# Joints between stages: norms, memory attention and a convolution re-ordered in a two-block transformer kernel

## The reference

```python
# first block
h = rmsnorm(x); q, k, v, gate = h @ w_in                 # two attentions of 8 heads each
y = [rmsnorm(forgetting_attention), rmsnorm(chunked_relpos_attention)]
x = x + rmsnorm(y @ w_out)
x = x + rmsnorm(softmax((rmsnorm(x) @ w_mq) K^T / 16) V @ w_mo)   # K, V from rmsnorm(mem), 256 rows, 4 heads
x = x + rmsnorm(square(relu(rmsnorm(x) @ w_ff1)) @ w_ff2)
# second block; c gives shift, scale and gate of every step (mod = silu(c) @ ada_w + ada_b)
h = modulate(rmsnorm(x)); a, g = split(h @ conv_in)
u = a * sigmoid(g); y = depthwise_conv(u, 31 taps) + b
x = x + gate * (silu(layer_norm(y)) @ conv_out)
x = x + gate * (square(relu(modulate(rmsnorm(x)) @ mlp1)) @ mlp2)
x = x + gate * hgrn2_mixer(modulate(rmsnorm(x)))         # gated linear recurrence, both directions
x = x + gate * (square(relu(...)) @ mlp2)
return rmsnorm(x)
```

## Time and profile before

| what | value |
|---|---|
| median of 3 runs | 2250.37 us (2248.27 to 2253.09) |
| profiled execution | 2249.68 us, its span 2247.7 us |
| PE busy | 2123.1 us (94%), 10732 matmuls |
| DVE / ACT / POOL busy | 1246.2 / 833.7 / 231.3 us |
| mean granted clock of PE | 0.983 |

### The profile page before, as it was taken

The page is one execution under the profiler, slowest core; times in us unless marked ns, Lnnn a source line. Parts: engine busy times, 40 slices in busy tenths (PEclk is TensorE's granted clock), DMA queues, the critical chain, the costliest instruction groups (busy, mean ns, idle before and its releaser), DMA issues.

```text
span 2247.7 us, 26801 instructions
## 1 busy us (share of the span) xinstructions
PE 2123.1 (94%) x10732; PEld 1658.6 (74%) x10732; DVE 1246.2 (55%) x1864; ACT 833.7 (37%) x1334; POOL 231.3 (10%) x189
## 2 busy tenths in 40 slices
PE   6999898899899999896999999999999989999998
PEld 5777786676778776563788888877767767888886
DVE  4455655427676776785553343456666665443443
ACT  4344544335332332313442232344454543332232
POOL 2221104014000003342100000100000001000001
PEclk9999999999999999998999999999999999999999
DMA  5212321122776773364232322221211132222321
GB/s 171 75 57 94 110 97 59 54 75 96 260 243 221 264 247 120 96 148 113 75 100 95 106 94 94 75 70 48 66 57 51 54 100 88 94 94 94 112 94 38
DMA packets 217531, 241.75 MB, mean 108 GB/s; under 512 B 9920, under 2 KB 203968, under 8 KB 211264
## 3 DMA queue, kind: packets, MB, share of 16 engines
q1 hardware_dynamic: 207232, 229.03, 31.3%
q10 hardware_dynamic: 10176, 11.00, 2.0%
HBM read 229.01 MB, written 2.10 MB: 103 GB/s over the span
## 4 chain that ended last, share of the span: by engine, by line
PE 80%; DVE 9%; ACT 6%; issue 2%; ACTq 1%; DMA 1%; POOL 1%; DVEq 0%; POOLq 0%
PE bank L1070 22%; PE bank L1071 21%; PE bank L1072 21%; PE bank L1091 2%; PE bank L1092 2%; PE bank L1093 2%; DVE wL L1636 1%; ACTq L1483 1%; PE bank L1263 1%; PE bank L1240 1%; PE bank L1196 1%; PE bank L1141 1%; DVE aacc L1804 1%; PE bank L1154 1%; ACT L1283 1%
## 5 line engine op out<-in xcount | busy, mean ns | idle before, releaser
L1070 PE MATMUL bank<-hH,wH 128*128 128x512 f32 (+1 forms) x1672 | 667.0, 399 | 41.0 <-DVE hL L1642 16.0
L1071 PE MATMUL bank<-hL,wH 128*128 128x512 f32 (+1 forms) x1672 | 649.8, 389 | 0.0
L1072 PE MATMUL bank<-hH,wL 128*128 128x512 f32 (+1 forms) x1672 | 649.7, 389 | 0.0
L1636 DVE TENSOR_TENSOR wL<-raw,wH 128x1024 fp32r<-128x1024 f32 (+1 forms) x342 | 384.6, 1166 | 162.3 <-ACT wH L1299 162.2
L1299 ACT ACTIVATE wH<-raw 128x1024 fp32r<-128x1024 f32 (+1 forms) x378 | 335.1, 937 | 373.9 <-PE bank L1072 279.8
L1070 PEld LDWEIGHTS bank<-hH,wH 128*128 128x128 f32 x1672 | 317.2, 190 | 136.9 <-issue 53.7
L1072 PEld LDWEIGHTS bank<-hH,wL 128*128 128x128 f32 x1672 | 317.2, 190 | 65.2
L1071 PEld LDWEIGHTS bank<-hL,wH 128*128 128x128 f32 x1672 | 317.4, 190 | 62.8 <-issue 2.9
L1070 PE MATMUL bank<-hidH,wH 128*128 128x512 f32 x768 | 300.5, 391 | 7.7 <-DVE hidL L1784 7.7
L1071 PE MATMUL bank<-hidL,wH 128*128 128x512 f32 x768 | 299.8, 390 | 0.0
L1072 PE MATMUL bank<-hidH,wL 128*128 128x512 f32 x768 | 299.7, 390 | 0.0
(11 more groups left out here) (204 smaller groups left out, 2072.0 us busy)
## 6 DMA issues: line engine op xcount, KB each, us to landing
raw<-in_mlp SPq DMA_DIRECT2D x64, 1024.0 KB, 5.3
araw<-in_ada_w SPq DMA_DIRECT2D x48, 1024.0 KB, 5.0
raw<-in_w_ff SPq DMA_DIRECT2D x32, 1024.0 KB, 7.3
raw<-in_hgrn_in SPq DMA_DIRECT2D x32, 512.0 KB, 3.8
raw<-in_w_in SPq DMA_DIRECT2D x12, 1024.0 KB, 5.3
u<-uc ACTq DMA_DIRECT2D x128, 67.5 KB, 3.3
raw<-in_conv_in SPq DMA_DIRECT2D x16, 512.0 KB, 4.8
raw<-in_w_mv SPq DMA_DIRECT2D x4, 1024.0 KB, 6.0
```

Of the source, the lines that this page charges most:

```text
L1070: mm(out, wh[:, k, m:m + 128], xh[:, k, 0:width], start=k == 0, stop=False)
L1071: mm(out, wh[:, k, m:m + 128], xl[:, k, 0:width], start=False, stop=False)
L1072: i = mm(out, wl[:, k, m:m + 128], xh[:, k, 0:width], start=False, stop=k == KB - 1)
L1636: e.tensor_tensor(wL[:, s, c], raw[:, r, c], wH[:, s, c].bitcast(F), SUB).then_inc(*s_wlo.up(n, x))
```

## The change

The parts, in the order of the list:

- *Memory squares.* The loads of mem and the eight squares with their additions stand before the k6 layer; the high and low parts stay behind it.
- *w_out and w_mo.* The last output block is squared from its bank. In `post_pre` all additions to x are on DVE; squares of blocks 0 to 3 are added by DVE between, those of 4 to 7 by POOL once the next layer has been asked for (`beside`).
- *Groups.* `fresh` is now a number; mq, ff1, mlp1, mlp2 and conv_out work their first four blocks (two pieces) together; the second piece's `take` does not look ahead. `hold=5` instead of 4 puts the norm's sum behind five blocks.
- *Memory attention.* A unit enters at each step (`stagger(..., 1)`) instead of four at a time.
- *First feed-forward.* A hidden block's low part is an item of its own, put behind the next block's first steps where several are pending; RM is 0.47 and the conditioning begins at -12.
- *Norm after the first feed-forward.* The root goes to a PSUM bank; four of the blocks are scaled into banks and added by DVE, blocks 0, 2, 4, 5 are added by POOL.
- *Convolution.* a and g of block 0 are worked together. For the last block half of the shifted copies are issued by SP, and only three DVE taps stand before the sum of block 6. The mean is of seven blocks; they are centred on it (0 to 2 by DVE, 3 to 6 by POOL) and squared before the eighth is there; the eighth is centred on the same mean, its sum (`rest`) corrects variance and blocks.

```diff
-RW, RM = 1.4, 0.44
+BY_POOL = (0, 2, 4, 5)
+RW, RM = 1.4, 0.47
-    def take(self, name, k0, c0, nc_):
+    def take(self, name, k0, c0, nc_, ahead=True):
...
-        while self.made < n + NSPLIT:
+        while ahead and self.made < n + NSPLIT:
...
+    def last_low(self):
+
+        if self.hidden is not None:
+            self.do("hidden_lo", **self.hidden)
+            self.hidden = None
...
+            group = fresh if c == 0 and fresh else 1
+            span = max(nc_, 128 * group)
+            ns = [self.take(name, k0, c0 + c + x, nc_, ahead=x == 0) for x in range(0, span, nc_)]
+            if self.beside is not None:
+                self.beside()
+                self.beside = None
...
+        if nxt is None:
+            rb, free = self.lin.get()
+            self.close(tag, 1024, busy=BUSY, out=(rb, free))
+            for j in range(KB):
+                pool = j in BY_POOL
+                z, free = (None, ()) if pool else self.lin.get()
+                self.do("post", tag=tag, src=src, j=j, rb=rb, z=z, after=free)
+                self.do("post_x", tag=tag, src=src, j=j, pool=pool, z=z)
...
+        else:
+            self.close(tag, 1024, busy=BUSY)
+            add = {}
+            for j in range(KB):
+                self.do("post", tag=tag, src=src, j=j, rb=None, z=None)
+                if j:
+                    self.do("pre_lo", tag=tag, nxt=nxt, j=j - 1)
+                self.do("post_x", tag=tag, src=src, j=j, pool=False, z=None)
+                self.do("pre_hi", tag=tag, nxt=nxt, j=j)
+                if j < 4:
+                    self.to_add = None
+                    self.square(nxt, j, ("xT", j), (self.x_event(tag, j),), by="dve")
+                    add[j + 2], self.to_add = self.to_add, None
+                if add.get(j) is not None:
+                    self.do("add_square", **add[j])
...
-                                   fresh=q == 0, hold=4)
+                                   fresh=4 if q == 0 else 0, hold=5)
...
+            for j in range(4):
+                do("mem", j=j)
+            yield from mem_squares()
             yield from self.linear("k6", "w_in", 0, 2312, 256, src, to_k(6), lag=True)
             yield from mem_kv()
...
+                if j == KB - 1:
+                    self.square(tag, j, ("bank", b), (("mm", "lin", t, j),), last=True)
                 do("ev_block", tag=tag, lin=t, j=j, b=b)
...
-        run(pipeline((munit(h, i) for h in range(4) for i in range(4)), 4))
+        run(stagger((munit(h, i) for h in range(4) for i in range(4)), 1))
...
-        run(weave(self.ffn("ff_pre", "w_ff1", 0, "w_ff2", 0, ("h", "ff_pre"), True, to_y), ada(), RM, start=-6.0))
+        run(weave(self.ffn("ff_pre", "w_ff1", 0, "w_ff2", 0, ("h", "ff_pre"), True, to_y), ada(), RM, start=-12.0))
...
+        def both():
+
+            ns = [self.take("conv_in", 0, c, 128, ahead=c == 0) for c in (0, 1024)]
+            parts = []
+            for n, t in zip(ns, "ag"):
+                b, free = self.lin.get()
+                parts.append(dict(n=n, m=0, b=b, after=free, key=("lin", (t, 0), 0), j=0))
...
+            else:
+                do("wdiag", blk=blk, k0=conv_first(blk), slot=slots[blk], after=free)
+                both()
             do("shift", blk=blk, slot=slots[blk], after=free)
             if blk:
                 b = taps_pe(blk - 1)
-            taps_dve(blk, range(5))
+            early = 5 if blk < KB - 1 else 3
+            taps_dve(blk, range(early))
...
+        taps_dve(KB - 1, range(3, conv_first(KB - 1)))
+        last = taps_pe(KB - 1)
+        vb, vfree = self.lin.get()
...
+        for j in (0, 3, 1, 4, 2, 5, 6):
+            do("ln_centre", j=j, s=s, pool=j > 2)
+            square_of(j)
+        do("conv_sum", blk=KB - 1, b=last, taps=conv_first(KB - 1))
...
+        do("ln_rest", b=db, after=free)
+        square_of(KB - 1)
+        do("ln_rest_square", b=db, s2=s2, free=free2)
+        do("ln_root", b=vb, s2=s2, rstd_free=self.rstd_free)
...
-                    for s in range(4):
+                    for s in range(4) if blk < KB - 1 else (0, 1):
...
+                elif kind == "shift" and it["blk"] == KB - 1:
...
+                    for s in (2, 3):
+                        for g in range(4):
+                            dma(u4[32 * s:32 * s + 32, x, g, :], uc[32 * g:32 * g + 32, blk, s:s + T + 28]).then_inc(
+                                s_u4[x], LANDED)
```

More of the change, by code:

```diff
@@ L205, in lows, with linear @@
         self.owed.clear()
-    def linear(self, tag, name, k0, c0, ncols, src, ev, width=T, nc_=256, before=None, lag=False, fresh=False, hold=1):
+    def linear(self, tag, name, k0, c0, ncols, src, ev, width=T, nc_=256, before=None, lag=False, fresh=0, hold=1):
         late = []
@@ L233, in linear @@
                         self.lows()
-                if m0 + 128 * group >= nc_:
-                    self.piece_done[n] = parts[-1]["key"]
+                for x, n in enumerate(ns):
+                    if m0 < nc_ * (x + 1) <= m0 + 128 * group:
+                        self.piece_done[n] = parts[-1]["key"]
                 if before is not None and len(late) + len(parts) >= hold:
@@ L270, in linear_tm, with square @@
                 yield 1.0
-    def square(self, tag, j, blk, after, last=False):
+    def square(self, tag, j, blk, after, last=False, by="pool"):
         if last:
@@ L419, in post_pre, with rest @@
             self.do("pre_lo", tag=tag, nxt=nxt, j=KB - 1)
-            for j in range(KB):
-                self.square(nxt, j, ("xT", j), (self.x_event(tag, j),))
+            def rest():
+                for j in range(4, KB):
+                    self.square(nxt, j, ("xT", j), (self.x_event(tag, j),))
+            self.beside = rest
         self.rstd_free = (("dve", "post", tag, KB - 1),)
     def x_event(self, tag, j):
-        ends = {"mix_post": True, "mem_post": True, "ff_post": False}
@@ L426, in x_event @@
-        if tag not in ends:
-            return ("dve", "x", tag, j)
-        pool = j > 0 if ends[tag] else j % 2 == 0
+        pool = tag == "ff_post" and j in BY_POOL
         return ("pool" if pool else "dve", "x", tag, j)
@@ L521, in to_gate @@
             return (("dve", "gate", 1),)
-        run(self.linear("q0", "w_in", 0, 0, 256, src, to_q(0), before=close_first, fresh=True, hold=2))
+        run(self.linear("q0", "w_in", 0, 0, 256, src, to_q(0), before=close_first, fresh=2, hold=2))
         run(self.linear("gate", "w_in", 0, 1536, 128, src, to_gate, nc_=128))
@@ L576, in ev @@
             def ev(t, j, b):
+                if j == KB - 1:
+                    self.square(tag, j, ("bank", b), (("mm", "lin", t, j),), last=True)
                 do("ev_block", tag=tag, lin=t, j=j, b=b)
-                self.square(tag, j, ("ymix", j), (("act", "y", tag, j),), last=j == KB - 1)
+                if j < KB - 1:
+                    self.square(tag, j, ("ymix", j), (("act", "y", tag, j),))
                 return (("act", "y", tag, j),)
             return ev
-        run(self.linear("w_out", "w_out", 0, 0, 1024, ("h", "y"), to_block("mix_post"), fresh=True))
+        run(self.linear("w_out", "w_out", 0, 0, 1024, ("h", "y"), to_block("mix_post"), fresh=2))
         self.post_pre("mix_post", "mem_pre", "ymix")
@@ L1201, in tensor_program @@
                         pe.wait_ge(*event(ev))
-                    mm(banks[it["b"]][:], ones, nacc[:], start=True, stop=False).then_inc(*s_mm.up("mean0"))
-                    pe.wait_ge(*s_dve.at("c", KB - 1))
-                    mm(banks[it["b"]][:], ones, yc[:, KB - 1, :], start=False, stop=True).then_inc(*s_mm.up("mean"))
+                    mm(banks[it["b"]][:], ones, nacc[:], start=True, stop=True).then_inc(*s_mm.up("mean"))
+                elif kind == "ln_rest":
+                    pe.wait_ge(*s_dve.at("cen", KB - 1))
+                    mm(banks[it["b"]][:], ones, yc[:, KB - 1, :], start=True, stop=True).then_inc(*s_mm.up("rest"))
                 elif kind == "ln_var":
+                    if it["first"]:
+                        for ev in it["after"]:
+                            pe.wait_ge(*event(ev))
                     pe.wait_ge(*s_act.at("csq", it["j"]))
-                    mm(banks[it["b"]][:], ones, tmp[:, it["s2"], :], start=it["j"] == 0, stop=it["j"] == KB - 1).then_inc(
+                    mm(banks[it["b"]][:], ones, tmp[:, it["s2"], :], start=it["first"], stop=it["last"]).then_inc(
                         *s_mm.up("var", it["j"]))
@@ L1868, in vector_program @@
                         *s_dve.up("c", blk))
-                elif kind == "ln_var":
+                elif kind == "ln_centre" and not it["pool"]:
                     j = it["j"]
@@ L2000, in pool_program @@
                             *s_wlo_pool.up(n, x))
-                elif kind == "square" and it["add"] is not None:
+                elif kind == "square" and it["add"] is not None and it["by"] == "pool":
                     pool.wait_ge(*s_act.at("sq", it["tag"], it["j"]))
```

247 lines of the change are left out of this document (155 added, 92 removed).

## The result

The changed kernel takes 2220.33 us (median of 4 runs, 2218.75 to 2221.82), the kernel before beside it 2251.73 (2248.27 to 2254.62): ratio 0.9861, 95% interval 0.9843 to 0.9879, so 31 us less. 2215 was forecast, in a range of 2203 to 2231. The profiled execution spans 2220.0 us at a mean clock of 0.982, against 2247.7.

A forecast was written before the change was run, and what follows sets the result against it. TensorE, busy 94% of the span, was taken as the bound, so only fewer matmuls or less standing and 1.2 GHz time help. Terms summed to 35.6 us off 2249.68: 2214.1, with 0.7 to the median 2215; range 2203 to 2231.

The forecast's parts named there:

- Memory squares: Before k6: squares and adds done under k6's matmuls remove TensorE's 6.84 us wait; gain 5.5 us, bounds 3 and 8.
- the 3 us that I took off: Behind k6: late copies to high and low parts and the attention step cost about 3 us of wait.
- Norms: After w_out and w_mo: no GpSimd additions, groups of four banks, TensorE sets the pace; net 6.0 us each, 12.0 together.
- Attention: Memory attention: one row entering per step lets scores cover the softmax, heads of 9.0 us; gain 7.0, bounds 3 and 9.
- With start=-12 ... gain 6.0: First feed-forward, first quarter's joint: conditioning begins after the quarter's 20 steps, removing two hidL waits of 3.0 us each.
- The surplus reappearing at three joints, 1.5 us: Later feed-forward quarters: 0.47 a step instead of 0.44 raises VectorE's demand; loss 1.5 us (0 to 8).
- the late sum: End of first feed-forward: last conditioning sum, its copy and DMA issues delay the norm's logarithm on ScalarE; loss 1.8 us.
- Rival B: First feed-forward: VectorE becomes the bound under 0.47, three joints of 3 to 5 us, norms low; 2230 us, chance 0.18.
- Outer norm: Norm after first feed-forward: VectorE operations with an operand in PSUM are not held up by GpSimd; gain 4.2 us.
- Start of the convolution: Block 0: g1's parts come behind 16 copy issues on ScalarE, TensorE stands 10 us; net -5.5 instead of +3.9.
- End of the convolution: Last block: copies from two queues 5.5 us sooner, norm 13.6 instead of 17.9 us; gain 9.7, bounds 5 and 12.
- rival C: Convolution: after the 10 us stand the clock stays at 1.2 GHz until its end; 77 us, 2292 us, chance 0.02.

The follow-up runs named there:

- the last run: Changed kernel with g1 asked for ahead of the copies, conditioning from -8.2, and mem's loads ahead of q6 (also "that with three"): 2201.4 us, ratio 0.9779.
- the version with two edits: Changed kernel with g1 asked for ahead of the copies and conditioning at 0.47 a step from -8.2 instead of -12: 2204.26 us, ratio 0.9782.

## Why the prediction was right, point by point

- *Memory squares*: right, 5.7 for 5.5, shown by the run that undoes them. What stays is not what I named (copies behind k6) but ScalarE's stand for the loads, which I had called harmless to TensorE; they cost 1 to 2 us, and some 2 more where the half clock follows. So the 3 us that I took off are met by luck, by another wait (2.2 us for PTb and the half clock behind it).
- *Norms*: 12.7 with the shortened w_out and w_mo stretches, for 12.0. Without the groups of four the gain of 5.6 a norm is gone, and taking the additions from GpSimd gives 0.1; whether the groups need that new order is not shown, as they were not run without it. Of "no hL waits" two are left, 1.15 us each at the first block. The 1.2 us for the logarithm was 0.8.
- *Attention*: right. A head takes 8.8 us, as forecast within 0.2 (3.5 + 0.9 + 3.5 is 7.9, not 7.8). The 8.5 us for 7.0 hold a phase of half clock that only the kernel before has; with it taken off the gain is 6.7.
- *First feed-forward*: the step that failed. "With start=-12 ... gain 6.0" gives nothing once the low parts come a block later, and that edit, which I did not cost, makes 5.4 of the 8.7 us. My 6.0 counted the two waits alone (2.96 and 2.91 us); the other 2.8 are the half clock that came with them (0.51 from 569 to 576 in the kernel before). "The surplus reappearing at three joints, 1.5 us" was 5.2, and not by density alone: the waits for aacc grew from 2.5 to 6.6 us, and behind both the clock was low (0.66 from 704 to 709 and from 810 to 815), some 1.6 us each, for which I had no term. At the same 0.47, started 3.8 earlier, 2.8 of the 5.2 go (4.3 where the clock stayed up, in the last run), and so does the late sum. Rival B's mechanism was at work here, at less than its price. The errors cancel, which is luck: 3.5 for 4.5.
- *Outer norm*: 3.3 for 4.2 (from the exponential's end at 866.91 to the logarithm at 878.01 are 11.1 us, forecast 10.1). Products and additions end at 875.21, after 8.3 us for 8.2 forecast; it is the tail that takes 2.8 us for 1.8, because the last blocks come together: three squares queue on ScalarE and six sums on TensorE, at a granted clock of 1.00 and 0.43 us a sum. Operands in PSUM make 3.0 of the gain, shown. The late sum was 1.4 for 1.8.

```profile
874.45 1.67 ACT L1428 ACTIVATE tmp<-xT 128x512 f32<-128x512 f32 x3 [0.66 <-POOL xT L2159]
...
875.13 2.84 PE L1206 MATMUL bank<-tmp,cst 128*128 128x512 f32 x6 [0.17 <-ACT tmp L1428]
```

- *Start of the convolution*: right in mechanism, place and size, -5.7 for -5.5, shown from both sides.
- *End of the convolution*: the norm 4.3 as forecast; the copies 4.1 for 5.5 (the stretch is 11.2 to 13.2 us in the other executions with two queues, so 3.2 to 5.2). SyncE does issue in 0.65 us like ScalarE; it was the landing that I had at about 2 us behind the last issue, where it is 4.7, although already had 4.3. The seven subtractions took 6.4 us on both engines together, between the prediction's 4.3 and 7.0 (VectorE's three took 1.36 us each, where one without GpSimd beside it takes 0.69), and as forecast that stayed under the conv matmuls.

```profile
1017.18 4.07 DVE L1988 TENSOR_TENSOR yc<-yc,tmp 128x512 f32<-128x512 f32 x3 [1.06 <-ACT tmp L1586]
1017.23 6.39 POOL L2170 TENSOR_TENSOR yc<-yc,tmp 128x512 f32<-128x512 f32 x4 [2.90 <-ACT tmp L1586]
```

- *Clock*: rival C did not come about; g1 ran at half clock for some 5 us, and block 6 was level again.

## What to carry to other kernels

A look-ahead that is switched off for one piece moves that piece's preparation to wherever the next request stands in its engine's queue: look at what is issued in between, DMA issues most of all. Work that is interleaved by steps moves when a loop is regrouped, even if its pace stays, so set its start anew. Two edits against the same stand overlap: undo each by itself before giving it a share.

## What the runs showed of the hardware

In a dense stretch, in which TensorE was busy for 20 of the 20 us before, the granted clock fell to 1.2 GHz for eight matmuls in one execution and stayed at 2.4 GHz at the same matmuls in another. First the changed kernel, then the kernel before (length, PE, PEld, DVE, ACT, POOL busy, clock, DMA share, GB/s):

```profile
60.00:80.00 20.00, 20.00 (x112) 16.42 (x111) 4.04 (x6) 4.67 (x8) 0.53 (x2) 1.00 0.35 105
80.00:90.00 10.00, 10.00 (x39) 7.58 (x38) 7.00 (x17) 3.59 (x10) 5.67 (x5) 0.83 0.35 106
```

```profile
60.00:80.00 20.00, 20.00 (x105) 16.09 (x104) 5.36 (x11) 5.93 (x9) 2.27 (x4) 1.00 0.27 85
80.00:90.00 10.00, 10.00 (x46) 7.22 (x45) 8.19 (x19) 2.15 (x10) 6.51 (x5) 1.00 0.35 106
```

Each such phase costs 1.5 to 1.7 us, and the executions differ in how many they have (matmul 1000 at 183.9 to 191.7). The same holds behind short stands. In the version with two edits and in that with three, TensorE stands 2.65 us for the same sum of the conditioning, and then has the low clock in the one and not in the other:

```profile
788.00:793.00 5.00, 4.46 (x16) 2.72 (x17) 2.35 (x4) 1.74 (x3) 0.00 (x0) 0.66 0.70 240
```

```profile
789.00:794.00 5.00, 4.47 (x23) 3.07 (x24) 2.35 (x4) 1.75 (x3) 0.00 (x0) 1.00 0.71 233
```

The Trainium skill, "TensorE: Matmul & The Clock Gate", HAM oscillation, ties the low clock to stands of TensorE between dense pieces; the stands of 9.3 us here bear that out each time, those of 1.7 to 2.7 us only in some executions, and the phases without a stand do not fit it. Why they come in one execution and not in another stays open.
